# Key and value compression with two positions of a block in one matmul, in a kernel whose buffers begin on a 128-byte line

## The reference, cut to what matters

```python
CMP_LEN = 32; CMP_STRIDE = 16; HEAD_DIM = 64; CMP_HIDDEN = 128; NSA_KV = 2

def compress(kv, pe, w1, w2):
    B, T, G, dh = kv.shape
    n_cmp = (T - CMP_LEN) // CMP_STRIDE + 1
    blk = np.arange(n_cmp)[:, None] * CMP_STRIDE + np.arange(CMP_LEN)[None, :]
    blocks = kv[:, blk] + pe[None, None, :, None, :]
    flat = blocks.transpose(0, 1, 3, 2, 4).reshape(B, n_cmp, G, CMP_LEN * dh)
    return jax.nn.gelu(flat @ w1) @ w2
```

## Time and profile before

| | |
|---|---|
| median of 3 runs | 1918.88 us (1916.68 to 1921.71) |
| profiled execution | 1921.35 us, span of its instructions 1919.5 us |
| TensorE matmul | 95% busy |
| TensorE weight load | 74% |
| VectorE | 49% |
| ScalarE | 36% |
| GpSimd | 7% |
| read from HBM | 168.33 MB, mean 89 GB/s |
| mean granted TensorE clock | 0.978 of full speed |

### The profile page before, as it was taken

The page is one execution under the profiler, slowest core; times in us unless marked ns, Lnnn a source line. Parts: engine busy times, 40 slices in busy tenths (PEclk is TensorE's granted clock), DMA queues, the critical chain, the costliest instruction groups (busy, mean ns, idle before and its releaser), DMA issues.

```text
span 1919.5 us, 27690 instructions
## 1 busy us (share of the span) xinstructions
PE 1828.1 (95%) x11652; PEld 1423.4 (74%) x11652; DVE 935.1 (49%) x1482; ACT 697.7 (36%) x1055; POOL 134.1 (7%) x109
## 2 busy tenths in 40 slices
PE   5998989989999998999999999899888899999999
PEld 2666655758888887788888887666688688888887
DVE  4276877364344343544344544545755544433442
ACT  4224557343223233432133334577311433312321
POOL 0013435200000002000000010000000010000000
PEclk8998998989999999999999999999999999999999
DMA  9662101113222223223223322111000122322241
GB/s 380 241 237 105 47 28 34 66 44 99 99 99 96 92 98 99 66 92 129 66 99 107 102 77 77 57 43 44 23 4 4 67 94 93 123 85 88 98 126 40
DMA packets 44475, 176.15 MB, mean 92 GB/s; under 512 B 5568, under 2 KB 5824, under 8 KB 41024
## 3 DMA queue, kind: packets, MB, share of 16 engines
q1 hardware_dynamic: 44352, 174.38, 26.8%
HBM read 168.33 MB, written 2.10 MB: 89 GB/s over the span
## 4 chain that ended last, share of the span: by engine, by line
PE 86%; DVE 7%; ACT 3%; DMA 3%; issue 2%; SPq 0%; DVEq 0%; ACTq 0%
PE bank L365 24%; PE bank L366 23%; PE bank L367 23%; PE bank L509 2%; PE bank L525 1%; PE bank L541 1%; PE bank L716 1%; DMA arena<-ada 1%; PE bank L857 1%; PE bank L874 1%; PE bank L865 1%; DMA arena<-ada_late 1%; PE bank L435 1%; DMA ring<-m_w_v 1%; ACT wsp L1088 1%
## 5 line engine op out<-in xcount | busy, mean ns | idle before, releaser
L1563 DVE TENSOR_TENSOR wsp<-ring,wsp 128x1024 fp32r<-128x1024 f32 (+2 forms) x244 | 313.7, 1287 | 442.6 <-ACT wsp L1088 442.5
L365 PE MATMUL bank<-hs,wsp 128*128 128x512 f32 x1160 | 473.1, 408 | 16.1 <-DVE hs L1830 5.3
L1088 ACT ACTIVATE wsp<-ring 128x1024 fp32r<-128x1024 f32 (+2 forms) x244 | 268.7, 1103 | 579.4 <-PE bank L367 573.7
L367 PE MATMUL bank<-hs,wsp 128*128 128x512 f32 x1160 | 455.5, 393 | 0.0
L366 PE MATMUL bank<-hs,wsp 128*128 128x512 f32 x1160 | 455.3, 393 | 0.0
L365 PEld LDWEIGHTS bank<-hs,wsp 128*128 128x128 f32 x1160 | 220.2, 190 | 87.4 <-issue 31.5
L366 PEld LDWEIGHTS bank<-hs,wsp 128*128 128x128 f32 x1160 | 220.3, 190 | 48.9 <-issue 5.9
L367 PEld LDWEIGHTS bank<-hs,wsp 128*128 128x128 f32 x1160 | 219.7, 189 | 47.2
L365 PE MATMUL bank<-hids,wsp 128*128 128x512 f32 x608 | 236.5, 389 | 0.0
L366 PE MATMUL bank<-hids,wsp 128*128 128x512 f32 x608 | 236.5, 389 | 0.0
L367 PE MATMUL bank<-hids,wsp 128*128 128x512 f32 x608 | 236.5, 389 | 0.0
(11 more groups left out here) (340 smaller groups left out, 2116.0 us busy)
## 6 DMA issues: line engine op xcount, KB each, us to landing
ring<-m_gate SPq DMA_DIRECT2D x44, 512.0 KB, 3.4
ring<-m_up SPq DMA_DIRECT2D x44, 512.0 KB, 3.4
ring<-m_down SPq DMA_DIRECT2D x32, 704.0 KB, 4.1
ring<-m_w_in SPq DMA_DIRECT2D x38, 512.0 KB, 3.5
arena<-ada_late SPq DMA_DIRECT2D x16, 1024.0 KB, 5.8
ring<-m_w_up SPq DMA_DIRECT2D x32, 512.0 KB, 3.4
ring<-m_w_down SPq DMA_DIRECT2D x32, 512.0 KB, 3.4
ring<-m_w_out SPq DMA_DIRECT2D x16, 512.0 KB, 3.6
```

What stands on the lines that cost most here:

```text
L365: pe.matmul(out, lhs[0], rhs[0], start=start, stop=False)
L367: return pe.matmul(out, lhs[1], rhs[0], start=False, stop=stop)
L1088: act.activation(wsp[:, s % SPLIT, 0, 0:size], ring[:, i % RING, 0:size], ACT.Copy)\
L1563: dve.tensor_tensor(wsp[:, s % SPLIT, 1, 0:size], ring[:, i % RING, 0:size], wsp[:, s % SPLIT, 0, 0:size].bitcast(F32), ALU.subtract).then ...
```

## The change

Two positions of a block, 2l and 2l+1, go on the two halves of the partitions, so that one product takes 128 useful rows, and 16 products replace 32. `blk` shrinks to half. For this, group 0 needs its odd positions on the upper partitions and group 1 its even positions on the lower ones: a new buffer `other_half` (in the room that `blk` leaves) takes a copy of the rows with the two halves of the partitions exchanged, by two DMAs of 64 partitions for each of key and value (`swap_halves`, on SP after the swap of tiles 4 and 5). Value's waits for the key blocks (`cmp_blocks`). GpSimd waits for these copies (`moved`) and fills `blk` with eight operations of 64 x 248 elements in place of four of 64 x 496. The weights come without their double, as two ring tiles of 512 KB in place of three of 704 KB, for key and value each. The position encodings take 16 columns each in place of 32, so `col` is 128 bytes per partition shorter and all that lies behind it, from `ext` on, begins 128 bytes lower. The stores at the end count on `moved` too.

```diff
-                  ("pe_k", 32), ("pe_v", 32)]:
+                  ("pe_k", 16), ("pe_v", 16)]:
...
-    out += [("w_in", n, 8 * P) for n in range(10)] + [("cmp1k", n, SLOT) for n in range(3)]
-    out += [("w_in", n, 8 * P) for n in range(10, 12)] + [("cmp1v", n, SLOT) for n in range(3)]
+    out += [("w_in", n, 8 * P) for n in range(10)] + [("cmp1k", n, 8 * P) for n in range(2)]
+    out += [("w_in", n, 8 * P) for n in range(10, 12)] + [("cmp1v", n, 8 * P) for n in range(2)]
...
-        blk = area(66 * K, (CMP_L, 2, CMP_N))
+        blk = area(66 * K, (CMP_L // 2, 2, CMP_N))
+        other_half = area(70 * K, (2, T))
...
-                for l in range(CMP_L):
-                    mm = pe.matmul(bank[:, 6, 2 * CMP_N * m:2 * CMP_N * (m + 1)], ws[l // 11][:, l % 11, :],
-                                   blk[:, l, :, :].rearrange("p g n -> p (g n)"), start=(l == 0), stop=(l == CMP_L - 1))
+                for l in range(CMP_L // 2):
+                    mm = pe.matmul(bank[:, 6, 2 * CMP_N * m:2 * CMP_N * (m + 1)], ws[l // 8][:, l % 8, :],
+                                   blk[:, l, :, :].rearrange("p g n -> p (g n)"), start=(l == 0), stop=(l == CMP_L // 2 - 1))
...
                 pool.wait_ge(S("roped"), src + 1)
+                pool.wait_ge(S("moved"), 32 * (m + 1))
                 if m:
                     pool.wait_ge(S("cmp_hid"), 1)
                 for half in range(2):
                     for g in range(2):
-
-                        rows = slice(DH * g, DH * g + DH)
-                        v = proj[rows, src, 16 * half:16 * half + 16 * 31].rearrange("p (n l) -> p l n", l=16)
-                        pe_b = vec(pe_name, 16 * half, 16)[rows, :, None].to_broadcast([DH, 16, 31])
-                        ins = pool.tensor_tensor(blk[rows, 16 * half:16 * half + 16, g, 0:31], v, pe_b, ALU.add)
-                        if half + g < 2:
-                            do(ins)
+                        for s in range(2):
+
+                            rows = slice(DH * s, DH * s + DH)
+                            v = proj[rows, src, :] if s == g else other_half[rows, m, :]
+                            v = v[:, 16 * half:16 * half + 16 * 31].rearrange("p (n l s) -> p l s n", l=8, s=2)[:, :, s, :]
+                            pe_b = vec(pe_name, 8 * half, 8)[rows, :, None].to_broadcast([DH, 8, 31])
+                            ins = pool.tensor_tensor(blk[rows, 8 * half:8 * half + 8, g, 0:31], v, pe_b, ALU.add)
+                            if half + g + s < 3:
+                                do(ins)
...
+            def swap_halves(m):
+                src = (KC, VC)[m]
+                sy.wait_ge(S("roped"), src + 1)
+                if m:
+                    sy.wait_ge(S("cmp_blocks"), 1)
+                for s in range(2):
+                    sy.dma_start(other_half[DH * s:DH * s + DH, m, :], proj[DH * (1 - s):DH * (1 - s) + DH, src, :])\
+                      .then_inc(S("moved"), 16)
+
...
-            after.update({3: ("cmp1k", 0), 4: ("cmp1k", 1), 5: ("cmp1k", 2), 6: ("w_in", 10), 7: ("cmp1v", 2),
+            after.update({3: ("cmp1k", 0), 4: ("cmp1k", 1), 5: ("w_in", 10), 6: ("w_in", 11), 7: ("cmp1v", 1),
...
                 if n != VC:
                     turn_halves(n)
+                if n - 1 in (KC, VC):
+                    swap_halves((KC, VC).index(n - 1))
                 if n in pieces:
                     late_load(pieces[n] + 1)
...
-        w1 = f["cmp_w1_" + name][0].reshape(CMP_L, DH, P).transpose(1, 0, 2)
-        w1 = np.concatenate([w1, w1], 0)
-        w1 = np.concatenate([w1, np.zeros((P, 1, P), np.float32)], 1)
-        mats["cmp1" + name] = np.ascontiguousarray(w1.reshape(P, 3, SLOT).transpose(1, 0, 2))
+        w1 = f["cmp_w1_" + name][0].reshape(CMP_L // 2, 2 * DH, P).transpose(1, 0, 2)
+        mats["cmp1" + name] = np.ascontiguousarray(w1.reshape(P, 2, 8 * P).transpose(1, 0, 2))
```

More of the change, by code:

```diff
@@ L477, in compress @@
             def compress(m):
-                ws = [take_whole("cmp1" + "kv"[m], "cmp_hid", m + 1).rearrange("p (l m) -> p l m", m=P) for _ in range(3)]
+                ws = [take_whole("cmp1" + "kv"[m], "cmp_hid", m + 1).rearrange("p (l m) -> p l m", m=P) for _ in range(2)]
                 pe.wait_ge(S("cmp_blocks"), m + 1)
@@ L2307, in _ @@
                 sy.wait_ge(S("x_added"), 4 * KD + n + 1)
-                sy.dma_start(out[:, n * T:(n + 1) * T], x[:, n, :]).then_inc(S("stored"), 16)
-            sy.wait_ge(S("stored"), 16 * KD)
+                sy.dma_start(out[:, n * T:(n + 1) * T], x[:, n, :]).then_inc(S("moved"), 16)
+            sy.wait_ge(S("moved"), 64 + 16 * KD)
 def columns(v):
@@ L2365, in lay_out @@
                                         "rw_ln_w_2", "rw_ln_b_2")]
-    cols += [np.concatenate([f["cmp_pe_" + n][0].T] * 2, 0) for n in ("k", "v")]
+    cols += [f["cmp_pe_" + n][0].reshape(CMP_L // 2, 2 * DH).T for n in ("k", "v")]
     cols = np.ascontiguousarray(np.concatenate(cols, 1))
```

## The result

The changed kernel takes 1932.72 us (median of 4 runs, 1931.46 to 1933.22), against 1917.78 us for the kernel before beside it (4 runs, 1913.96 to 1921.71): a ratio of 1.0076, 95% interval 1.0057 to 1.0094. It is 0.8% slower, where 0.2% faster was forecast, and it lies 13 us above the end of the forecast's range, 1919.8. The profiled execution took 1931.46 us with a span of 1929.7 us; the span is 10.2 us over that of before.

What follows compares the result with a forecast made beforehand. TensorE, 86% of the chain, was taken to bound the kernel. Key -3.6, value 0, and loads, GpSimd and SP 0 summed to -3.6 us: 1915.3 us against the median 1918.9, range 1911.0 to 1919.8.

Steps and rivals of the forecast that it cites:

- Part (e): Constants shrink, so everything from ext on begins 128 bytes lower, off 256-byte lines; no engine minds, cost nothing.
- Rival 4: Transfers into arena and tmp, off the 256-byte line, become slower by 0.8 to 1.0 us: about 1916.2; chance 0.05.
- The matmuls: Each compression on TensorE: 64 instructions become 32 at the same 112 ns, 3.58 us, losing 3.6 us.
- Where the first 3.6 us go: Key compression's saving passes whole through VectorE's first mask (153.1) to n = 10, starting at 165.0; -3.6 us.
- Step (d): GpSimd's additions under VectorE's top rounds and tile 7's rope: steps lose at most 2.4 us, covered by room; cost 0.
- Where the second 3.6 us go: Value compression's saving meets TensorE's wait for VectorE's masks; counted as 0, bounds 0 and 3.6.
- (a), (b), (c): Swaps take SP 1.2 us, GpSimd's eight additions 6.4 us, a late load may stall TensorE 0.6 us; sum 0.
- list of "wrong" signs: Late-load stall over 2 us between 118 and 132, key's blocks after 116.5, n = 10 at 161.5 or over 167.
- rival 3: SP held by the new wait: slow additions make key's blocks, swap and late load late; +1.4 us, 1920.3; chance 0.06.
- Rival 1: Both compressions' savings pass, as VectorE's slack lets TensorE run on: -7.2 us, 1911.7; chance 0.12.
- rival 5: Matmuls' time is not halved because an instruction with both halves filled is slower; 1918.9; chance 0.02.
- Rival 2: More TensorE idle before n = 10 brings the low clock again or longer: 1917.0 to 1918.7; chance 0.17.

Runs made afterwards that it cites:

- e7: Kernel before with wsp alone moved 128 bytes off a 256-byte boundary; 1950.42 us, ratio 1.0162.
- e3: Kernel before with ext and tmp 128 bytes off a 256-byte boundary and arena on one; 1921.72 us, ratio 1.0011.
- e13: Kernel before with everything behind x 128 bytes further; 1919.52 us, ratio 1.0001.
- e5: Kernel before with arena and the small buffers behind it 64 bytes further; 1931.37 us, ratio 1.0063.
- e6: Kernel before with arena and the small buffers behind it 32 bytes further; 1940.08 us, ratio 1.0103.
- e2: Kernel before with arena and the small buffers behind it 128 bytes off a 256-byte boundary; 1938.2 us, ratio 1.0098.
- e11: Kernel before with both wsp and arena 128 bytes off a 256-byte boundary, hs on one; 1938.86 us, ratio 1.0095.
- e14: Changed kernel at 256 bytes, value swap later on SP's queue, value's blocks in a room of their own, filled earlier; 1912.73 us, ratio 0.9968.
- e9: Changed kernel at 256 bytes with the 16 value products issued twice, putting back the time saved; 1917.82 us, ratio 0.9991.
- e1b: Changed kernel with ext, tmp and arena rounded to 256 bytes, run again beside its variants; 1916.05 us, ratio 0.9977.
- e1: Changed kernel with ext, tmp and arena rounded to 256 bytes instead of 128; 1914.19 us, ratio 0.9975.
- e10: Changed kernel at 256 bytes with the 16 key products issued twice; 1920.71 us, ratio 1.0002.
- e8b: Changed kernel at 256 bytes with the value swap later on SP's queue, second group of runs; 1914.39 us, ratio 0.9976.
- e12: Kernel before with hs, ring, wsp, constants and arena 32 bytes off a 256-byte boundary, ext and tmp on one; 1921.87 us, ratio 1.0007.

## Why the prediction was wrong, step by step

**Part (e), the addresses: the step that failed.** It put the shift of 128 bytes at nothing, because the earlier trace rows gave "no sign that an engine minds where a row begins". Those 22 matmuls have 348 columns, and none of the 2520 products that the shift touches was among them. No fp32r product of 512 columns stood in the trace of before with its two operands at different residues (fp32r is the type of the rounded parts that `hs`, `hids` and `wsp` hold), so the 6.65 ns that they lose, 2.9% of their distance, could not be read there.

The earlier trace rows was also read in the wrong quantity. It gives durations, and products overlap; a cost of a few ns shows in the distance of two starts. The rows of 348 columns in a weight tile begin at 0, 112, 224 and 80 bytes modulo 256. TensorE's timeline of before has the first products of the second, third and fourth row, and the last product of the fourth:

```profile
53.84 0.32 PE L365 MATMUL bank<-wsp,hs 128*128 128x348 f32 x1
...
55.72 0.32 PE L365 MATMUL bank<-wsp,hs 128*128 128x348 f32 x1
...
57.62 0.32 PE L365 MATMUL bank<-wsp,hs 128*128 128x348 f32 x1
...
59.37 0.32 PE L367 MATMUL bank<-wsp,hs 128*128 128x348 f32 x1
```

The twelve distances of the second row take 1.88 us, 156.7 ns each, and eleven of the fourth take 1.75 us, 159.1 ns, with a granted clock of 1.00 from 52.0 to 59.6. The last 46 distances of that tile take 7.27 us in all, and 7.32 us in e7, where `wsp` lies 128 bytes further. So distances that differ by row were there to be seen, as a reason to doubt. They are no proof of the same effect: the row whose operands agree modulo 256, the first, takes 158.2 ns and is not the fastest.

What did stand there was a count: TensorE with 86% of the chain, and most of it in one shape whose two operands shared one residue modulo 256 and after the change no longer did, in 2520 cases. An unknown with no row that fits should have had a price at both ends: 1% of 2520 products at 227 ns is 5.7 us, more than the whole expected gain. Rival 4 named the 256-byte line, but put its cost on transfers and at 1 us. The cost was on TensorE, 16.8 us by the distances. Transfers show none: the first loads into `arena`, 17.39 us on the chain before, take 17.12 us after; the late load landed after 4.9 us, as in the earlier trace rows; and e3 and e13 are at 1.0011 and 1.0001 of before. For that rival I had leaned on the Trainium skill (DMA: Bandwidth & Descriptors, "How a descriptor splits into AXI transactions"); its table has one transaction more for 576 bytes that start off 256 and none for 96, and no run here shows a time for the further transaction.

The Trainium skill has a rule on operand addresses (SBUF — State Buffer, section "Operand start alignment"): an operand may begin at any multiple of its element size. Starts at 32, 64 and 128 bytes, as it allows, are what e5, e6 and e2 have, and they add what the rule leaves out: on TensorE, 32 bytes between the two operands' residues cost 1.0% of this kernel (e6).

**The cause behind the addresses is not shown.** The trace gives one hint. In a window at 560 us the next product's weights are loaded while a product runs; of the kernel after, the weight loads:

```profile
559.85 0.19 PEld L366 LDWEIGHTS bank<-hids,wsp 128*128 128x128 f32 x1
560.08 0.19 PEld L367 LDWEIGHTS bank<-hids,wsp 128*128 128x128 f32 x1
```

They begin within 0.01 us of a matmul's start (559.84 and 560.08), so two streams of reads run at once, and e11 says that only their relative place counts. That the two reads get in each other's way is an argument, not a measurement. Why 64 bytes slow one product of three nearly fully and one not at all is open.

**Other shapes.** No experiment was built for them, but the traces hold some. Plain fp32 products with 128x128 weights out of the constants and 512 columns out of `arena` hardly change: those of L423 of before, whose operands agree modulo 256, have a mean of 590 ns, and a median of 590 ns in after and 591 in e6, 128 and 32 bytes off. The products of the compression read `ring` and `arena` and keep their distance of 112 ns in after, with 128 bytes between the two. What the runs show holds for fp32r products of 512 columns.

**The matmuls (right).** 32 instructions took 3.79 and 3.76 us, where 3.58 us and the last one's drain were expected.

**Where the first 3.6 us go (right in place, short in size).** GpSimd's timeline of after, 109 to 148:

```profile
109.14 7.27 POOL L2214 TENSOR_TENSOR arena<-arena,col 64x248 f32<-64x248 f32 x8 [59.33 <-DMA arena<-arena]
137.94 7.56 POOL L2214 TENSOR_TENSOR arena<-arena,col 64x248 f32<-64x248 f32 x8 [21.53 <-PE bank L485]
145.58 2.13 POOL L2227 TENSOR_TENSOR arena<-tmp,arena 128x512 f32<-128x512 f32 x1
```

VectorE's timeline of after, 146 to 155, with its index scores (L1668) and its first mask (L1733):

```profile
146.51 2.63 DVE L1668 SCALAR_TENSOR_TENSOR arena<-tmp,widx,arena 128x512 f32<-128x512 f32 x2
...
154.40 0.69 DVE L1733 CUSTOM_DVE_ANT_0 arena<-bank,cst 128x512 f32<-128x512 f32 x1 [0.20 <-DVE arena L1682]
```

GpSimd's eight additions last until 145.5, and its rope of tile 8 (145.58) meets the index scores, which take 2.63 us. Before they took 1.62 (at 149.85), and the forecast kept that: 1.0 us more. So the first mask is at 154.40, where 153.1 was forecast, and n = 10 at 166.21, not 165.0. Step (d) had counted such meetings for the rope of tile 7 alone and covered them with VectorE's idle time; it did not ask what a GpSimd that ends at 145.5 does next. e14 moved the meeting and got half of it back.

**Where the second 3.6 us go (right up to n = 10).** TensorE waits 1.69 us for VectorE's mask before the scores of 155.16, and e9 shows the value at 0 there. By n = 11 e9 is 2.5 us behind e1b, so 0 for the whole kernel is open.

**(a), (b), (c): swaps, additions, SP's wait (sizes too small, sum not shown).** The chain of after in order of time, 102 to 123:

```profile
102.21 6.76 DMA arena<-arena
109.14 0.74 POOL arena L2214
...
113.99 1.62 POOL arena L2214
...
116.50 0.50 SPq L2291
...
118.20 4.93 DMA arena<-ada_late
123.18 1.06 PE bank L436 x8
```

The key swap landed after 6.76 us, not 4.0; late loads of 1 MB each, issued at 100.25 and 104.19, were under way beside it, which is the likely reason. One addition took 0.74 us (0.8 forecast) with 0.07 us to the next, and one was held to 1.62 by VectorE. The key blocks were there at 116.42 (114.2 forecast), the swap that waits for them 1.4 us after SP was free for it, and the late load came at 118.20 and held TensorE 2.48 us, where 0.6 was forecast. The list of "wrong" signs named over 2 us. This is rival 3's mechanism at a small size. The key compression starts at 133.99 for 133.90, and the later stall of 0.91 us is gone, so the sum of this part, 0, looks right. That is in part luck. TensorE was some 1.8 us earlier at 103 than before; the granted clock from 40 to 76 us was 0.90 where it had been 0.83, which can account for it. And one pair of traces can't tell it: the same code started its first key product at 133.83 in e1 and at 135.48 in e1b, and the kernels with the old compression did so between 131.9 and 135.4. Of these ten the mean is 133.2, of the five with the new one and the first queue order (after, e1, e1b, e9, e10) 134.3. So the cost may be about 1 us, inside the forecast's +1.5.

**The rivals.** Rival 1 (both pass) is excluded by e9 up to n = 10, rival 5 (no halving) by the timeline. Rival 2 (the clock): between 100 and 300 us the mean granted clock is 0.96 in both, so it cost nothing that a row can tell (0.01 of that stretch is 2 us). In e1 and e1b it went the other way from the rival, and helped; see "The sum". That stretch of before, with the columns of the earlier trace rows:

```profile
100.00:300.00 200.00, 186.46 (x1254) 124.27 (x1253) 151.04 (x440) 90.46 (x229) 70.52 (x65) 0.96 0.28 95
```

and of after, where the clock is again the third number from the end:

```profile
100.00:300.00 200.00, 181.93 (x1209) 118.94 (x1205) 153.05 (x448) 93.00 (x236) 76.23 (x74) 0.96 0.26 86
```

**The sum.** With the 256-byte line, which removes the loss that (e) missed, the ratio is 0.9975 and 0.9977 in two groups of runs: -4.8 and -4.3 us, where -3.6 was forecast. The intervals of the two ratios reach from -8.2 to -1.5 us and from -7.1 to -1.9 us. That the medians lie near the forecast is in part luck, because the traces add them up from other terms. Up to n = 10 the change gains 2.4 us. Up to n = 11 it gains 5.0 in e1 and e1b (52.12 and 52.15 us for 57.14), and the same in e8b (51.94), but 2.3 in the kernel after (54.85). In e1, e1b and e8b TensorE's granted clock is 0.57, 0.62 and 0.59 from 156 to 164 us, ahead of TensorE's wait for n = 10, and back at 1.00 when n = 10 begins. In before it is 0.51 from 168.5 to 172, and in after 0.52 from 166.5 to 170, with n = 10 under way. So 2.6 of the 5.0 us go with the place of the low clock, a term that rival 2 had with the opposite sign; nothing here shows that the change brings it about.

## What to carry to other kernels

A buffer that shrinks moves everything behind it. Before a change, list the start addresses of both operands of each frequent matmul modulo 256, before and after; if their difference changes, pad, or move all of them together. To see such a cost in a trace, take the distance of starts over a long run of products, not the busy time. And an instruction time saved on the busiest engine is worth its size only up to that engine's next wait: here one of two equal savings arrived at the next tile of the projection and the other did not.

## What the hardware showed unexpectedly

- 128x128 by 512-column fp32r products on TensorE start 226.6 ns apart when stationary and moving operand begin at the same residue modulo 256 bytes, and 233.3 ns apart when one lies 128 bytes off, at a granted clock of 1.00 (before and after, 191 distances each).
- Only the difference counts: both 32 or both 128 off cost nothing (e12, e13).
- At 64 bytes the three products of a weight took 394, 392 and 388 ns on average, for 389 at 0 and 395 at 32 and 128 (e5, e6, e2).
- Plain fp32 products of 512 columns had the same 590 ns with and without the 128 bytes (L423 of before, L424 of after).
- A copy of 64 partitions by 2 KB took 6.8 us to land while megabyte loads were under way, and two engines' elementwise operations (VectorE's and GpSimd's) held each other up by 0.5 to 1.0 us where these traces show them meeting (index scores 2.63 us for 1.62, an addition 1.62 for 0.74, a split 1.84 for 1.29).
